# Recurrent layer: order of forget gates, scores and first levels in the first two head pairs; a square root ahead of its use; own PSUM bank for a turn

## The reference, cut to what matters

```python
u = h @ w_in;  q, fz, i, gate = jnp.split(u, 4, axis=-1)
log_f = jnp.logaddexp(jnp.log(lbf), jnp.log1p(-lbf) + jax.nn.log_sigmoid(fz))
k = (1.0 - lbf) * jax.nn.sigmoid(-fz)
A = jnp.einsum('bhtd,bhsd,bhtsd->bhts', qc, kc, jnp.exp(diff))   # diff: decay between s and t, t >= s
o = einsum('bhts,bhsv->bhtv', A, vc) + ...                       # across chunks through the state S
o = o * rsqrt(mean(o * o) + EPS) * norm_g;  y = (o * silu(gate)) @ w_out
...
hc = _rmsnorm(ctx, norm1_g) * (1 + scale_c) + shift_c            # second block, then hc @ w_in[:, k and v]
```

## Time and profile before

| | us |
|---|---|
| median of 3 runs (968.0 to 968.44) | 968.11 |
| the profiled execution's own time | 966.77 |
| its span in the trace | 965.5 |
| PE busy | 874.7 (91%) |
| DVE busy | 602.7 (62%) |
| ACT busy | 433.7 (45%) |

### The profile page before, as it was taken

How to read it: one execution, slowest core, us unless ns; L and a number is a source line. 1 busy time by engine, 2 the same in 40 slices (tenths; PEclk the granted TensorE clock), 3 DMA queues, 4 the chain that set the end, 5 groups by cost and what they waited for, 6 DMA issues and landing times.

```text
span 965.5 us, 13498 instructions
## 1 busy us (share of the span) xinstructions
PE 874.7 (91%) x5523; PEld 751.5 (78%) x5523; DVE 602.7 (62%) x846; ACT 433.7 (45%) x659; POOL 47.9 (5%) x72
## 2 busy tenths in 40 slices
PE   5999999989799999999999789496679599999995
PEld 4978878659799999999887689383347499999994
DVE  7644444434767797778866554598554666666564
ACT  6445334236255635645535433234544354444432
POOL 8100000001000000000000000600000000000000
PEclk9999999999799999999999799797789699999998
DMA  8878788883344444345336216530006155555531
GB/s 289 283 268 298 275 292 287 322 262 125 95 131 129 133 131 132 112 150 175 126 118 225 88 44 172 153 131 0 1 0 218 44 174 178 198 192 175 178 127 44
DMA packets 101446, 156.43 MB, mean 162 GB/s; under 512 B 11284, under 2 KB 67960, under 8 KB 98312
## 3 DMA queue, kind: packets, MB, share of 16 engines
q1 hardware_dynamic: 101384, 155.56, 48.8%
HBM read 154.44 MB, written 1.11 MB: 161 GB/s over the span
## 4 chain that ended last, share of the span: by engine, by line
PE 76%; DVE 10%; ACT 5%; DMA 4%; issue 3%; SPq 2%; DVEq 0%; POOL 0%; ACTq 0%; POOLq 0%
PE acc L406 10%; PE acc L407 10%; PE acc L408 10%; PE acc L432 8%; PE acc L433 7%; PE acc L434 7%; PE misc L980 5%; PE misc L750 2%; PE misc L1844 2%; PE misc L1845 2%; PE misc L1846 2%; DVE w_lo L379 2%; ACT w_hi L372 2%; PE acc L1597 2%; PE misc L1584 1%
## 5 line engine op out<-in xcount | busy, mean ns | idle before, releaser
L379 DVE TENSOR_TENSOR w_lo<-raw,w_hi 128x2048 fp32r<-128x2048 f32 x115 | 262.8, 2296 | 222.6 <-ACT w_hi L372 222.5
L372 ACT ACTIVATE w_hi<-raw 128x2048 fp32r<-128x2048 f32 x115 | 219.5, 1910 | 150.9 <-PE misc L1846 28.1
L406 PE MATMUL acc<-XH,w_hi 128*128 128x256 f32 x848 | 244.1, 288 | 2.9 <-ACT KT L1464 2.8
L407 PE MATMUL acc<-XL,w_hi 128*128 128x256 f32 x848 | 242.0, 285 | 0.0
L408 PE MATMUL acc<-XH,w_lo 128*128 128x256 f32 x848 | 241.8, 285 | 0.0
L406 PEld LDWEIGHTS acc<-XH,w_hi 128*128 128x128 f32 x848 | 165.0, 195 | 6.8 <-ACT KT L1464 3.0
L407 PEld LDWEIGHTS acc<-XL,w_hi 128*128 128x128 f32 x848 | 165.0, 195 | 0.8
L408 PEld LDWEIGHTS acc<-XH,w_lo 128*128 128x128 f32 x848 | 164.7, 194 | 0.0
L432 PE MATMUL acc<-w_hi,XH 128*128 128x512 f32 (+1 forms) x224 | 88.4, 395 | 0.0
L434 PE MATMUL acc<-w_hi,XL 128*128 128x512 f32 (+1 forms) x224 | 86.1, 384 | 0.0
L433 PE MATMUL acc<-w_lo,XH 128*128 128x512 f32 (+1 forms) x224 | 86.0, 384 | 0.0
(11 more groups left out here) (259 smaller groups left out, 1327.1 us busy)
## 6 DMA issues: line engine op xcount, KB each, us to landing
raw<-in_hgrn_w_in_dram SPq DMA_DIRECT2D x32, 1024.0 KB, 5.5
ada_raw<-in_ada_w_dram SPq DMA_DIRECT2D x24, 1024.0 KB, 5.0
raw<-in_ffn_w_up_dram SPq DMA_DIRECT2D x22, 1024.0 KB, 5.1
raw<-in_pool_w_in_dram SPq DMA_DIRECT2D x16, 1024.0 KB, 7.7
raw<-in_ffn_w_down_dram SPq DMA_DIRECT2D x11, 1024.0 KB, 4.9
raw<-in_w_in_dram SPq DMA_DIRECT2D x10, 1024.0 KB, 5.2
raw<-in_pool_w_out_dram SPq DMA_DIRECT2D x8, 1024.0 KB, 7.3
raw<-in_hgrn_w_out_dram SPq DMA_DIRECT2D x8, 1024.0 KB, 5.1
```

The costliest lines, as they stand in the source:

```text
L372: self.hi_done.up(act.activation(self.w_hi[v % RING][:, 0:w], self.raw[j][:, 0:w], ACT.Copy), v)
L379: self.lo_done.up(dve.tensor_tensor(self.w_lo[j][:, 0:w], self.raw[j][:, 0:w], self.w_hi[v % RING][:, 0:w].bitcast(F32), ALU.subtract), v)
L406: pe.matmul(o, wh[:, k, c:c + P], xh[:, k, :], start=k == 0, stop=False)
L407: pe.matmul(o, wh[:, k, c:c + P], xl[:, k, :], start=False, stop=False)
```

## The change

Four edits.

1. In pair 1 PE runs the scores of pair 0, head 0, behind the forget gates of pair 1 instead of ahead of them. Other pairs keep their order.
2. In pair 0 DVE runs `levels(0)` ahead of `lo` of forget + 4 instead of behind it.
3. The fourth turn of "ctx" goes to bank 1 and does not wait for the first piece's remainder.
4. In `act_out` ACT takes a square root of one column (result unused) after the first column half of the pooling output, ahead of the `hi` units of the second.

```diff
     BANKS = (0, 2, 3, 0)
+    BANKS_OF = {"ctx": (0, 2, 3, 1)}
+
+    def turn_bank_of(self, name, half, c):
+        return self.misc[self.BANKS_OF.get(name, self.BANKS)[2 * half + c]]
     def pe_turn(self, name, half, c, src):
         pe.wait_ge(self.V.h, self.V["scaled", name, half, c])
-        if n == 3:
+        if n == 3 and name not in self.BANKS_OF:
             pe.wait_ge(self.V.h, self.V["xl", name, 0, 0])
...
             if c == 0:
                 self.hi(self.first(u0, 3) + RING)
+
+                self.A.up(self.nc.scalar.activation(self.eps[:, 1:2], self.eps[:, 0:1], ACT.Sqrt, bias=0.0))
...
                 self.project(self.u_query[p], h, h * P, X, KD, ...)
-            if p:
+            if p > 1:
                 self.pe_scores_of(p - 1, 0)
...
             for h in range(2):
                 self.project(self.u_forget[p], h, h * P, X, KD)
+            if p == 1:
+                self.pe_scores_of(0, 0)
             if p:
                 self.pe_scores_of(p - 1, 1)
...
+            if p == 0:
+                self.levels(0)
             self.lo(self.first(forget) + RING)
             if p:
                 self.dve_scores_of(p - 1, 1)
-            if q is not None:
-                self.dve_heads_low(q, 1)
-            self.levels(p)
+                if q is not None:
+                    self.dve_heads_low(q, 1)
+                self.levels(p)
```

More of the change, by code:

```diff
@@ L530, in pe_turn, with turned @@
         pe.wait_ge(self.V.h, self.V["scaled", name, half, c])
-        if n == 3:
+        if n == 3 and name not in self.BANKS_OF:
             pe.wait_ge(self.V.h, self.V["xl", name, 0, 0])
         for k in range(4):
-            m = pe.transpose(self.misc[self.BANKS[n]][:, k * P:k * P + P],
+            m = pe.transpose(self.turn_bank_of(name, half, c)[:, k * P:k * P + P],
                              src[:, half, (4 * c + k) * P:(4 * c + k + 1) * P], self.ident[:, :])
         self.T.up(m, "turned", name, half, c)
-    def turned(self, half, c):
-        return self.misc[self.BANKS[2 * half + c]][:, :].rearrange("p (k t) -> p k t", k=4)
+    def turned(self, name, half, c):
+        return self.turn_bank_of(name, half, c)[:, :].rearrange("p (k t) -> p k t", k=4)
     def act_high(self, name, half, c, hi):
@@ L543, in act_high @@
         act.wait_ge(self.T.h, self.T["turned", name, half, c])
-        self.A.up(act.activation(hi[:, 4 * c:4 * c + 4, half * P:half * P + P], self.turned(half, c), ACT.Copy),
+        self.A.up(act.activation(hi[:, 4 * c:4 * c + 4, half * P:half * P + P], self.turned(name, half, c), ACT.Copy),
                   "xh", name, half, c)
@@ L549, in dve_low @@
         dve.wait_ge(self.A.h, self.A["xh", name, half, c])
-        self.V.up(dve.tensor_tensor(lo[:, k, t], self.turned(half, c), hi[:, k, t].bitcast(F32), ALU.subtract),
+        self.V.up(dve.tensor_tensor(lo[:, k, t], self.turned(name, half, c), hi[:, k, t].bitcast(F32), ALU.subtract),
                   "xl", name, half, c)
```

## The result

| | before | after |
|---|---|---|
| median, us | 968.11 (5 runs, 966.87 to 969.69) | 962.84 (5 runs, 962.44 to 964.33) |
| ratio, with 95% interval | | 0.9947 [0.9932, 0.9961] |
| profiled execution, us | 966.77 | 962.95 |
| span, us | 965.5 | 961.7 |

The change makes the kernel 5.3 us faster; the forecast was 5.6 us (962.5). A second measurement of the same kernel gave 962.47 us, ratio 0.9932 [0.9908, 0.9957].

The account below looks back on a forecast made before the run. PE, busy 91% of the span, was taken to bound the kernel, its stalls paid twice through the clock. Edit 4's 1.3, edits 1 and 2's 1.3 and edit 3's 3.0 sum to 5.6 us: 968.11 to 962.5, 8-in-10 range 956.8 to 965.8.

Parts of the forecast that it names:

- PE's wait for XN: PE's 3.2 us wait for the first normalised piece of "out" would become 1.9 us with the early square root.
- remainders hidden with 2.0 us to spare: Three remainders (6.7 us) behind levels(0) on DVE end at 256.1; DVE's next duty, head 0's scores, comes at 258.1.
- stall 3.7 us: Between scores of heads 0 and 1, PE idles 258.1 to 261.8 for DVE's picks, ACT's two copies and hand-overs.
- pair gain 1.3: Edits 1 and 2 together gain 6.6 us, less 4.5 to 6.4 for the fallen clock; 1.3 taken.
- the half clock on the wide columns: Wide columns behind head 1's scores would run slow for 3.2 to 5.1 us, costing 1.6 to 2.6 us.
- The rival of the kept clock: Clock stays up in the new stall, edits 1 and 2 give 6.6 us, time 957.2 (956 to 959); chance 0.2.
- the old stall's 10.3: Price of PE's wait at 248.65 for levels(0): 4.9 us idle, plus 3.8 and 1.6 us lost at half clock.
- PE's wait ahead of the rows: In the context stage, PE waits 2.3 us for the remainders (HCL), done by 540.3, before doing the rows.
- the addition without its wait: DVE's addition, standing for PE until 544.77, would follow its remainder at once at 542.5, 2.3 us earlier.
- the last scaled piece of "in2": On DVE, done at 557.2 instead of 560.87, 3.7 us earlier with edit 3.
- The token tile's half clock: Tiles behind in2's last turn run slow for 2.9 to 5.1 us, before 2.9: 0 to 1.1 us more, middle 0.6.
- Slower, by the clock downstream: In the attention, the shift puts more score batches at half clock, 1.8 us each; four give 969.7, five 971.5; chance 0.06.

Follow-up runs that it names:

- the second trace: Profile of the kernel with all four edits, unchanged, measured a second time: 962.47 us, ratio 0.9932 to the kernel before.
- the filled kernel: The kernel with all four edits, plus 30 dense matmuls (results overwritten) behind pair 0's first scores, where PE would idle: 960.86 us, ratio 0.991.

## Why the prediction was right

The forecast of 962.5 was met to 0.3 us. The mechanisms hold, but the closeness is partly luck, since the terms don't add up so well when each is measured by itself. On the kernel before, edit 3 alone gives 3.1 us and edit 4 alone nothing (0.3 us slower); edits 3 and 4 together give 5.8 (969.08 to 963.28), and all four 5.3 and 5.6. So in the medians edits 3 and 4 gave the whole of it, and of the 1.3 us of edits 1 and 2 little or nothing is seen.

**Edit 4** (forecast 1.3, bounds 0.8 and 1.8). The trace has 1.54 at the first projection where the clock stayed at 1.00 through the turns, and 1.2 where it didn't (6.48 in the table). The load measured 1.28 us again at its new place, and PE's wait for XN fell from 3.23 to 2.17 us (forecast 1.9). The Trainium skill (ScalarE: Activation LUTs, "What ACT_TABLE_LOAD costs") adds a drain of about 1.4 us to the load. It isn't seen in this case: before, the load ends at 213.94 + 1.28 = 215.22, and the root starts 0.02 us behind it.

```profile
215.24 0.29 ACT L503 ACTIVATE nstat<-nstat 128x1 f32<-128x1 f32 x1
```

What I missed is that this gain doesn't reach the end by itself: alone, it is nothing in the median. In the sum of the four it can't be told from the other terms.

**Edit 2** (levels 4.0 us earlier, remainders hidden with 2.0 us to spare). Levels at 239.34, 0.03 us behind the factors; DVE's slack 2.13 us. Right. The prediction priced edits 1 and 2 as a pair and did not say that with edit 1 in place edit 2 is worth nothing, though its own numbers had it (levels due at 253.4, forget gates over at 254.3).

**Edit 1** (forget gates to 254.3, stall 3.7 us, clock falls, pair gain 1.3, bounds 0.2 and 2.1). Scores from 254.4, stall 3.68 us, half clock on all of head 1's scores. What the pair gained is not settled within the forecast's bounds: at pair 1's first scores the trace says 2.15 us and the second trace 0.7 (75.32 against 77.58, less edit 4's 1.54); against edits 3 and 4 alone they say 3.6 and 2.1; the medians say 0.4 and 0.8. One cause is the length of the half clock on the wide columns, forecast at 3.2 to 5.1 us and measured at 1.2 and 4.3. The rival of the kept clock, at 957.2, did not happen, and the filled kernel shows that it had the mechanism right: fill the stall and the clock stays at 1.00. Of the 5.3 us that this rival had beyond the forecast, the filled kernel shows 3.5 at pair 1's first scores (73.89 - 70.44) and 1.6 to 2.0 in the medians.

The working missed what it pointed to. With edit 2 alone the old order would have stalled for 0.8 us and no clock would have fallen: 9.5 us of the old stall's 10.3 were to be had (the table has 77.44 - 68.45 = 9.0 at pair 1's first scores), and with edit 1 only 3.6 of them came in one trace (77.44 - 73.89) and 2.1 in the other. All the terms stood in the prediction; the comparison of the two orders did not.

**Edit 3** (forecast 3.0, bounds 2.5 and 3.6). Alone it gives 3.1 us. Its parts: PE's wait ahead of the rows 2.44 us (forecast 2.3), the addition without its wait, the last scaled piece of "in2" is done at 554.25 + 0.69 = 554.94 instead of 560.87, 5.9 us earlier, of which 2.2 had come before (the remainder ahead of the context's scaling begins at 519.88, before at 522.12): 3.7, as forecast. The token tile's half clock is longer, 4.9 us against 2.9.

**Slower, by the clock downstream** (0.06). It didn't happen to the whole change, but something like it did to edit 4 alone. That kernel lost 1.4 us behind the first token tile and 1.6 from the DMA of rpb to the end of the attention. In the attention itself one batch of scores took 3.45 us instead of 2.51, and its PE busy time there was 51.9 us at a clock of 0.77 instead of 50.0 at 0.81. The forecast priced such a batch at 1.8 us and looked at the attention alone.

## What to carry to other kernels

Before moving work ahead of a stall, ask what that work was covering: the forget gates covered the round trip between two batches that share PSUM banks, and taking them away made a new stall of 3.7 us of waiting and 4.1 us of clock, nearly as dear as the 10.3 us of the one removed. If two edits attack one stall, price each alone: on top of edits 3 and 4, edit 2 brought 6.9 us (963.28 to 956.38), and edits 1 and 2 together 0.4 (to 962.84), at most 2.6 by the traces' ends. Give each piece of a turn its own bank wherever one is free: three such banks gave 3.1, 2.1 and 1.4 us in the medians, the last two with intervals that overlap.

## What the runs showed of the hardware that was not expected

A gain early in the kernel can vanish later without any engine's work changing. Edit 4 alone was 2.3 us ahead at the first token tile and 1.1 us behind at the end of the span (754.12 against 753.02). In between PE idled no more than before; the same matmuls took longer, since more of their time fell into stretches at 1.2 GHz (56.3 us against 53.4). Two executions of one and the same kernel differed by 1.4 us at one point for the same reason. And in the filled stall the clock was worth 4.1 us beside 3.7 us of waiting, so that matmuls whose result is thrown away cost nothing and by the median gained 1.6 to 2.0 us, though the intervals of the two ratios overlap. The same batch of scores ran through in 3.8 us at 1.00 where the clock was up, and in 7.6 us at 0.50 where it had fallen, in this stall as in the old one.
